# A decoder trunk on one core: four edits in the second attention joined, transposes moved, lambda loaded as columns, x ahead of the biases

## The reference

```python
mod = c_act @ ada_w[layer] + ada_b[layer]            # six vectors of 2048 for each layer
shift_t, scale_t, gate_t, shift_m, scale_m, gate_m = jnp.split(mod, N_MOD, axis=-1)
h = modulate(rms_norm(x, norm_g[layer, 0]), shift_t, scale_t)
# layer 0: dilated window attention; layer 1: differential attention on shared K and V
lam = jnp.exp(jnp.sum(lp[0] * lp[1])) - jnp.exp(jnp.sum(lp[2] * lp[3])) + lam_init
a = p[:, :, 0] - lam * p[:, :, 1]
x = x + gate_t[:, None, :] * y
h = modulate(rms_norm(x, norm_g[layer, 1]), shift_m, scale_m)
x = x + gate_m[:, None, :] * sq_relu_mlp(h, mlp_w1[layer], mlp_w2[layer])
```

## Time and profile before

| | us |
|---|---|
| median of 3 runs | 2373.57 (2373.55 to 2374.35) |
| profiled execution | 2374.41 |
| its span, first to last instruction | 2372.6 |
| PE busy in it | 2342.0 |
| VectorE busy | 1768.1 |
| ScalarE busy | 1242.7 |

### The profile page before, as it was taken

How to read it: one execution, slowest core, us unless ns; L and a number is a source line. 1 busy time by engine, 2 the same in 40 slices (tenths; PEclk the granted TensorE clock), 3 DMA queues, 4 the chain that set the end, 5 groups by cost and what they waited for, 6 DMA issues and landing times.

```text
span 2372.6 us, 28881 instructions
## 1 busy us (share of the span) xinstructions
PE 2342.0 (99%) x11309; PEld 1937.5 (82%) x11309; DVE 1768.1 (75%) x2291; ACT 1242.7 (52%) x2162; POOL 52.7 (2%) x74
## 2 busy tenths in 40 slices
PE   7999999999999999999999999999999999999999
PEld 4468888888888888888888888877888888888887
DVE  6678878888999878888898887858875555555554
ACT  3166566667535534534546666654653553553542
POOL 1000000001000000000001210000100000000000
PEclk9999999999999999999999999999999999999999
DMA  9987777966999888798886877657875555555554
GB/s 393 424 333 297 303 293 300 379 233 248 368 397 367 331 301 336 290 342 307 328 338 235 340 298 271 240 179 277 323 277 195 187 191 192 192 189 195 187 193 153
DMA packets 151000, 665.38 MB, mean 280 GB/s; under 512 B 17392, under 2 KB 17872, under 8 KB 121424
## 3 DMA queue, kind: packets, MB, share of 16 engines
q1 hardware_dynamic: 150864, 663.53, 75.0%
HBM read 661.33 MB, written 2.13 MB: 280 GB/s over the span
## 4 chain that ended last, share of the span: by engine, by line
PE 87%; DMA 5%; DVE 5%; ACT 3%; issue 1%; POOL 1%; SPq 0%; DVEq 0%; ACTq 0%
PE main L533 18%; PE main L428 16%; PE main L430 16%; PE main L429 16%; PE main L535 9%; DMA qT<-ada 3%; PE main L442 2%; PE main L444 2%; PE main L443 2%; DVE w_lo L1335 1%; DVE ada_raw L1342 1%; DMA subg_sb<-subg 1%; DVE qT L1342 1%; PE tr L584 1%; PE tr L533 1%
## 5 line engine op out<-in xcount | busy, mean ns | idle before, releaser
L906 ACT ACTIVATE w_hi<-w_raw 128x1024 fp32r<-128x1024 f32 x771 | 793.8, 1055 | 548.1 <-DMA w_raw<-w 545.0
L1335 DVE TENSOR_TENSOR w_lo<-w_raw,w_hi 128x1024 fp32r<-128x1024 f32 x771 | 921.6, 1220 | 213.1 <-ACT w_hi L906 211.0
L1342 DVE CUSTOM_DVE_ANT_0 ada_raw<-ada_raw,c_row,biasc 128x2048 f32<-128x2048 f32 x208 | 492.0, 2365 | 31.2 <-DMA ada_raw<-ada 30.0
L533 PE MATMUL main<-hT,w_hi 128*128 128x512 f32 x1856 | 464.7, 392 | 0.0
L533 PEld LDWEIGHTS main<-hT,w_hi 128*128 128x128 f32 x1856 | 334.3, 189 | 60.1
L428 PE MATMUL main<-w_hi,mid_hi 128*128 128x512 f32 x960 | 373.5, 389 | 0.0
L429 PE MATMUL main<-w_lo,mid_hi 128*128 128x512 f32 x960 | 373.5, 389 | 0.0
L430 PE MATMUL main<-w_hi,mid_lo 128*128 128x512 f32 x960 | 373.4, 389 | 0.0
L428 PE MATMUL main<-w_hi,hT 128*128 128x512 f32 x848 | 338.7, 399 | 1.8 <-ACTq L950 0.8
L430 PE MATMUL main<-w_hi,hT 128*128 128x512 f32 x848 | 330.8, 390 | 0.0
L429 PE MATMUL main<-w_lo,hT 128*128 128x512 f32 x848 | 330.1, 389 | 0.0
(11 more groups left out here) (270 smaller groups left out, 1884.2 us busy)
## 6 DMA issues: line engine op xcount, KB each, us to landing
w_raw<-w SPq DMA_DIRECT2D x800, 512.0 KB, 4.4
ada_raw<-ada SPq DMA_DIRECT2D x208, 1024.0 KB, 6.8
qT<-ada SPq DMA_DIRECT2D x16, 1024.0 KB, 12.3
gate<-gate_rows SPq DMA_DIRECT2D x4, 1024.0 KB, 8.3
xs<-x SPq DMA_DIRECT2D x1, 2048.0 KB, 7.6
out<-xs SPq DMA_DIRECT2D x3, 512.0 KB, 6.5
out<-xs SPq DMA_DIRECT2D x2, 256.0 KB, 2.6
st_a<-lamb SPq DMA_DIRECT2D x1, 256.0 KB, 17.9
```

The lines of the kernel that those rows point to most:

```text
L533: pe.matmul(banks[f][:, :], w_hi[:, s, wc], hT[:, :, kt, :], start=(kt == 0), stop=False)
L906: act.activation(w_hi[:, s, :], w_raw[:, s, :], ACT.Copy).then_inc(hi_done, 1)
L1335: dve.tensor_tensor(w_lo[:, s, :], w_raw[:, s, :], w_hi[:, s, :].bitcast(F32), ALU.subtract).then_inc(lo_done, 1)
L1342: dve.tensor_tensor_reduce(piece, piece, c_row[:, :], gain, biasc[:, section, kt:kt + 1], ALU.mult, ALU.add, out).then_inc(ada_used, 1)
```

## The change

**Second attention.** (1) No dots stand in V0 (`ADA_Q`, fifth list), V9 has three instead of two, V10 and V11 two each instead of three, and chunk B4 gets four (`ADA_GATE_B`). In the stream of dots all sections behind that move with them, so gate 2 is written and read in V4 instead of V2, and gate 3 in B4 and B5 instead of B4 (SyncE's `gate_steps`). The squares that ScalarE makes in Q3, for the norm of Q2's result (`qk_stats`, `ch == 3`), go to the banks `sc` and `ov` instead of `st_b`, and POOL waits for one root fewer before it writes `st_b`: the one in Q2 instead of the one in Q3. (2) `heads[2:4]` and `lows[2:4]` stand ahead of the split of piece V8.4 instead of behind it. (3) PE's transposes of heads 4 and 5 stand behind V8.2 instead of V8.1. (4) The table of the square root is loaded by an operation of its own ahead of `sub_stats` in V9.

**First chunks.** The first `qk_transposes` in A2 stand behind piece 2 instead of piece 1. x is loaded ahead of the biases. Lambda comes as 128 partitions by 4 elements; VectorE multiplies pairs, PE sums over the partitions with a matmul of `ones`, VectorE copies the two sums, and the two reductions in `angles` are gone. VectorE's last two copies of `c_row` stand ahead of the bias operations.

```diff
-ADA_Q = after((), (0, 5, 7), (0, 5, 7), (0, 5, 7), (0, 3, 6), (0, 5, 7), (0,))
-ADA_V = after((6, 7), (5, 7), (0, 6), (5, 7), (0, 6), (1, 2), (), (5, 6), (4, 5, 6), (0, 2, 5), first=2)
-ADA_GATE_B = after((1, 3, 5, 7), (0, 2, 4, 6), (0, 2, 4, 6))
+ADA_Q = after((), (0, 5, 7), (0, 5, 7), (0, 5, 7), (), (0, 5, 7), (0,))
+ADA_V = after((6, 7), (5, 7), (0, 6), (5, 7), (0, 6), (1, 2), (), (4, 5, 6), (4, 5), (0, 2), first=2)
+ADA_GATE_B = after((1, 3, 5, 7), (0, 2, 4, 6), (0, 2, 4, 6), (0, 1, 3, 4))
...
             sp.dma_start(cols_in[0:96, :], vecs_in).then_inc(vec_in, 16)
+            sp.dma_start(xs[:, :, :], x_in.rearrange("(t p) d -> p t d", p=P)).then_inc(x_in_done, 16)
             sp.dma_start(biasc[:, :, :], bias_cols_in).then_inc(bias_in, 16)
-            sp.dma_start(xs[:, :, :], x_in.rearrange("(t p) d -> p t d", p=P)).then_inc(x_in_done, 16)
+            sp.dma_start(lamb4[:, :], lamb_in).then_inc(lamb_in_done, 16)
...
-            sp.dma_start(st_a[:, 0:NC], lamb_in.partition_broadcast(P)).then_inc(small_in, 16)
...
-            gate_steps = {2: {3: lambda: gate_write(2), 6: lambda: gate_read(2, 4 + 16)}}
+            gate_steps = {4: {3: lambda: gate_write(2), 6: lambda: gate_read(2, 4 + 16)}}
...
-            gate_steps = {3: {1: lambda: gate_write(3), 4: lambda: gate_read(3, 4 + 16 + 4)}}
+            gate_steps = {3: {7: lambda: gate_write(3)}, 4: {1: lambda: gate_read(3, 4 + 16 + 4)}}
...
             spread_c()
+            pe.wait_ge(lamb_paired, 1)
+            claim_tr(0)
+            pe.matmul(tr[0][:, 0:2], ones[:, :], lamb2[:, :], start=True, stop=True).then_inc(lamb_summed, 1)
...
-                gemm(0, *h, side={1: [qk_transposes], 5: [qk_transposes]})
+                gemm(0, *h, side={2: [qk_transposes], 5: [qk_transposes]})
...
-                                  1: [head_transposes(4, heads), head_transposes(5, heads)],
+                                  2: [head_transposes(4, heads), head_transposes(5, heads)],
...
-                chunk(PIECES, {4: [qk_stats(1 - ch % 2)], 5: [qk_scale(1 - ch % 2)],
+                chunk(PIECES, {4: [qk_stats(1 - ch % 2, places=(sc, ov) if ch == 3 else None)], 5: [qk_scale(1 - ch % 2)],
...
-            chunk(PIECES, {3: heads[0:2], 4: [values(1), exps_of(0), exps_of(1)], 5: heads[2:4], 6: heads[4:6], 8: [move_pt]})
-            chunk(PIECES, {1: [sub_stats], 2: [sub_stats], 4: [heads[6]], 5: [heads[7]]})
+            chunk(PIECES, {3: heads[0:2], 4: [values(1), exps_of(0), exps_of(1), *heads[2:4]], 6: heads[4:6], 8: [move_pt]})
+            chunk(PIECES, {1: [load_sqrt, sub_stats], 2: [sub_stats], 4: [heads[6]], 5: [heads[7]]})
...
+            for q in range(2, 4):
+                dve.wait_ge(c_wide, q + 1)
+                dve.tensor_copy(c_row[:, cols(q, NC)], c_banks[q][:, :]).then_inc(c_spread, 1)
             dve.wait_ge(bias_in, 16)
...
-            for q in range(2, 4):
-                dve.wait_ge(c_wide, q + 1)
-                dve.tensor_copy(c_row[:, cols(q, NC)], c_banks[q][:, :]).then_inc(c_spread, 1)
+            dve.wait_ge(lamb_in_done, 16)
+            dve.tensor_tensor(lamb2[:, :], lamb4[:, 0::2], lamb4[:, 1::2], ALU.mult).then_inc(lamb_paired, 1)
+            dve.wait_ge(lamb_summed, 1)
+            dve.tensor_copy(lam[:, 0:2], tr[0][:, 0:2]).then_inc(tr_free[0], 1)
...
-                dve.wait_ge(small_in, 16 * 2)
-                lm = st_a[:, 0:NC].rearrange("p (a b) -> p a b", a=4)
-                dve.tensor_tensor_reduce(gate_flat[:, 0:P], lm[:, 0, :], lm[:, 1, :], 1.0, 0.0, ALU.mult, ALU.add, lam[:, 0:1])
-                dve.tensor_tensor_reduce(gate_flat[:, P:2 * P], lm[:, 2, :], lm[:, 3, :], 1.0, 0.0, ALU.mult, ALU.add,
-                                         lam[:, 1:2]).then_inc(lam_dot, 1)
+                dve.wait_ge(small_in, 16)
...
-            section_chunk(8, {2: [causal[0], negate_max(0)], 3: lows[0:2], 4: [causal[1], negate_max(1)], 5: [*lows[2:4], mix(0)], 6: [*lows[4:6], mix(1)],
+            section_chunk(8, {2: [causal[0], negate_max(0)], 3: lows[0:2],
+                              4: [causal[1], negate_max(1), *lows[2:4]], 5: [mix(0)], 6: [*lows[4:6], mix(1)],
...
-            modulate_kept((S_SCALE_KV, S_SHIFT_KV), 4 * PIECES, 4 * GROUPS + 3)
+            modulate_kept((S_SCALE_KV, S_SHIFT_KV), 4 * PIECES, 4 * GROUPS + 2)
```

More of the change, by code:

```diff
@@ L212, in trunk @@
         turns = sb("turns", [P, T * HALF])
+        lamb4 = sb("lamb4", [P, 4])
+        lamb2 = sb("lamb2", [P, 2])
         scratch = sb("scratch", [P, 1])
@@ L217, in trunk @@
         pos_i = sb("pos_i", [P, T], I32)
-        sb("skip", [P, 192])
+        sb("skip", [P, 186])
         with nc.sbuf_tensor("mid_hi", [P, KT, T * P], F32R) as mid_hi, \
@@ L263, in trunk @@
         ada_used = sem("ada_used")
+        lamb_in_done, lamb_paired, lamb_summed = sem("lamb_in_done"), sem("lamb_paired"), sem("lamb_summed")
         c_ready, c_wide, c_spread = sem("c_ready"), sem("c_wide"), sem("c_spread")
@@ L1679, in _ @@
             chained(last)
-            for q in range(2, 4):
-                dve.wait_ge(c_wide, q + 1)
-                dve.tensor_copy(c_row[:, cols(q, NC)], c_banks[q][:, :]).then_inc(c_spread, 1)
+            dve.wait_ge(lamb_in_done, 16)
+            dve.tensor_tensor(lamb2[:, :], lamb4[:, 0::2], lamb4[:, 1::2], ALU.mult).then_inc(lamb_paired, 1)
+            dve.wait_ge(lamb_summed, 1)
+            dve.tensor_copy(lam[:, 0:2], tr[0][:, 0:2]).then_inc(tr_free[0], 1)
+            dve.wait_ge(tr_free[0], 3)
+            dve.sem_inc(lam_dot, 1)
             dve.wait_ge(c_spread, 4)
@@ L2040 @@
         "subg": f["b_subln_g"].reshape(-1),
-        "lamb": f["b_lambda"].reshape(-1),
+        "lamb": f["b_lambda"].reshape(4, HD).T,
         "ada": np.concatenate([w.reshape(-1, D) for w in (first, *by_column[2:])]),
```

## The result

The changed kernel takes 2383.96 us (median of 5, 2382.15 to 2385.09) against 2373.57 (median of 5, 2372.58 to 2374.35): a ratio of 1.0043, 95% interval 1.0033 to 1.0054. It is 10.4 us slower. The prediction was 2362.2 with a range of 2359.5 to 2367.0, so it was wrong in sign and by 21.8 us.

A forecast was written before the change was run, and what follows sets the result against it. PE's work, taken as fixed, plus time in which PE starts no matmul bounds the kernel. Gains 1.2 + 1.6 + 1.6 + 1.4 + 1.2 + 4.4 = 11.4 us off 2374.4, less 0.84 for the median, give 2362.2 (2359.5 to 2367.0).

The forecast's parts named there:

- A: Start: smaller lambda load frees transfer time in the first stage; gain 1.2 us (-1.4 to 1.8), 1.05 by the 512 B rule.
- C: V0 to V1.1: no dots in V0 and POOL starting earlier regain 1.6 of 1.97 us lost, at least 0.8.
- F: V11: a dot less each in V10 and V11 removes PE's waits and the slow clock's 1.7; 4.4 us (1.0 to 4.8).
- B: A2: transposes one piece later remove PE's wait for the rope's last product; 1.6 us, or 0.4.
- D: V8: lows of heads 2 and 3 earlier, transposes of heads 4 and 5 later, remove PE's wait; 1.4 us, or 0.9.
- E: V9: square root table loaded ahead removes PE's wait for the seventh head's scaling; 1.2 us, or 0.8.
- R1: Rival, V9: SyncE stands at the block behind the added dot, weights land late, V9.7 waits; costs 4.0 us (2366.2), chance 0.17.
- R2: Rival: first stage is bound by its slots, so the later first dot makes A -1.4 us (2364.8); chance 0.10.
- R4: Rival, B4 to B5: gate 3 lands late and B5's first update waits, making the kernel slower (2379); chance 0.03.

The follow-up runs named there:

- e1: The changed kernel with filler `skip` at 170 elements instead of 186, so mid_hi and what follows start at the addresses of the kernel before; 2363.01 us, ratio 0.9955.
- e9: e1 with lambda loaded (256 KB to all partitions) and reduced as in the kernel before, x still ahead of the biases; 2365.26 us, ratio 0.9964.
- e12: e7 with the first qk_transposes of A2 behind piece 1 again instead of piece 2; 2361.01 us, ratio 0.9951 to the kernel before.
- e7: e1 with the added dot of V9 behind V9.0 instead of V9.4; 2360.59 us, ratio 0.9944 to the kernel before.
- e13: e7 with the dots' tables, places of the squares, POOL's root and the gates' places as in the kernel before; 2368.24 us, ratio 0.9977.
- e11: e7 with heads and lows 2 and 3 behind the split, transposes of heads 4 and 5 behind V8.1, the table loaded at the root; 2363.17 us, ratio 0.9959.
- e14: The kernel before with `skip` 16 elements shorter (176 instead of 192), mid_hi and mid_lo 64 bytes nearer to the weights; 2380.51 us, ratio 1.0027.
- e15: The kernel before with `skip` 48 elements longer (240 instead of 192), mid_hi and mid_lo 192 bytes further from the weights; 2380.22 us, ratio 1.0026.

## Why the prediction was wrong

**The step that failed** is in its first paragraph: "the time is PE's work plus the time in which PE doesn't start a matmul, and an edit on another engine is worth only what it takes out of that". The first summand was held fixed at 0.227 us for 512 columns. The change moved it to 0.233 for 3072 matmuls through two buffers of 16 and 8 bytes. No rival had it; "that the change doesn't do what it says has no room, since the order shows each edit" is the sentence that closed the door, for an order of instructions shows no address. The material was there: two new buffers and a filler whose only use is to place what follows, changed by the sum of their sizes. The range, 7.5 us wide, was made of waits alone. What the runs showed in its place: the 3072 matmuls on `mid_hi` and `mid_lo` cost 20.3 us more by their starts, 21 by e1. With the addresses right the time is 2363.0 (e1) against 2362.2. That it comes so near is in part luck, since errors of both signs cancel: A and C with F brought some 2.7 us more than forecast, B some 1 less, and the new wait cost 2.4.

Term by term, with the addresses right:

| term | forecast | measured | by |
|---|---|---|---|
| A, lambda | 1.2 (-1.4 to 1.8) | 2.25 | e9 against e1 |
| B, A2 | 1.6 (0.4 to 1.6) | 0.4 | e12 against e7 |
| C and F | 6.0 | 7.65 | e13 against e7 |
| D and E | 2.6 | 2.6 (2.9 between the traces) | e11 against e7 |
| R1, new wait | 0 (chance 0.17, 4.0) | -2.4 (-3.9 between the traces, with the clock's fall in e1) | e1 against e7 |
| placement | not seen | -21 | e1 against the changed kernel |

**A** was right in its mechanism and too small. The loss of rate was 1.2 us in one window, and I bounded the rest by lambda's own bytes; the trace of e9 shows a reduced rate in the window before too. From 16 to 20 us, e9 and then e1:

```profile
16.00:20.00 4.00, 2.19 (x10) 2.19 (x11) 3.96 (x6) 0.19 (x2) 0.00 (x0) 0.50 0.91 367
16.00:20.00 4.00, 1.34 (x6) 1.34 (x7) 3.96 (x6) 0.07 (x1) 0.00 (x0) 0.50 0.99 406
```

The two windows lack (39 + 124) GB/s x 4 us = 0.65 MB, or 1.5 us at 426 GB/s, and with the 0.6 of lambda's own bytes that makes 2.1 of the 2.25. R2 falls: the first dot came later (11.99 in the trace after, 13.11 in e1's, 11.77 before) without cost. I also read a row wrongly: 0.60 for "x5" is the time of all five bias operations, not of one; after, the same group takes 0.51. And the biases are 112 KB in the profile, not some 40. The sum for the delay came out near all the same: counted from the first copy of c_row, the first dot starts 1.44 later than before (3.24 against 1.80), through two hand-overs of 0.48 and 0.40 that I hadn't priced.

```profile
10.25 0.51 DVE L1686 SCALAR_TENSOR_TENSOR biasc<-biasc,vec 128x16 f32<-128x16 f32 x5
10.79 0.16 DVE L1690 TENSOR_TENSOR lamb<-lamb 128x2 f32<-128x2 f32 x1
11.43 0.16 DVE L1692 COPY lam<-tr 128x2 f32<-128x2 f32 x1 [0.48 <-PE tr L771]
11.99 2.35 DVE L1348 CUSTOM_DVE_ANT_0 ada_raw<-ada_raw,c_row,biasc 128x2048 f32<-128x2048 f32 x1 [0.40 <-DMA ada_raw<-ada]
```

The Trainium skill ("DMA: Bandwidth & Descriptors", Specifications) has 512 B as the least transfer for line rate. Here 2 KB in rows of 16 B took 7.2 us to land behind x's 2 MB, which cost the stage nothing visible, so no run tests the 0.15 us between 1.05 and 1.2; the measured 2.25 is above both.

**B** was wrong in size: the wait went, and most came back as PE had to wait later: 0.6 at 190 us for a split, and by the starts 0.3 more near 463 us, where the profile names no wait. The prediction asked what is late next for other terms and answered it here only up to the transposes' own users.

**C** was the full 1.95 of its bound in the trace after. **D** and **E** were right within the noise: 1.6 and 1.3 between the traces of e11 and e7, against 1.4 and 1.2. By the Trainium skill ("ScalarE: Activation LUTs", What ACT_TABLE_LOAD costs) E could have been worth up to 2.66. The trace doesn't agree: before, the load starts at 1581.17 and takes 1.28, and the root follows at once,

```profile
1582.47 0.30 ACT L1021 ACTIVATE rmsv<-ssv,eps_t 128x2 f32<-128x2 f32 x1
```

so the row's 1.28 was the price that counted.

**F** was right in place and cause, and measured 5.2 against 4.4. The addition of 1.7 for the clock was right in number by luck: e13 and e15 lose as much with a full clock, to a third wait of 1.7. The prediction took a fall of the clock as a cost of its own, without asking whether the next split was there.

**R1** happened, as a neighbour of what was written. SyncE did stand at the block (16.1 us) and the weights did come late. But the split of V9.7 was still in time; what was late was the update behind the splits of V10. The prediction held the chance at 0.17 against a margin of 0.2 us that it had worked out itself. Its price of 4.0 is met only where the clock falls too (3.9 in e1's trace).

R4 didn't happen; PE had no wait in B5.

## What to carry to other kernels

Before waits are counted, compare the start addresses of all buffers in the two built programs, and ask which matmuls read a pair whose distance changed. Before a slow clock is priced, ask whether what the engine needs next would have been there. A filler is kept right by the sizes as allocated (here 32 bytes for a buffer of 8), not by the sizes as written. And of a stream with two slots: a step put late into an idle chunk holds up whoever asks for the slot after the next, so a step belongs into the first idle time, not the last.

## What the runs showed of the hardware that I had not expected

- The pace of a matmul of 128x128 by 512 columns depends on where its two operands lie in the on-chip memory relative to each other. By the change of their distance modulo 256 bytes it was 226.8 ns at 0, 233.3 at 32 and 64, 232.4 at 128, 228.9 at 192 (in the last case 225.9, 229.1 and 231.7 for three kinds of pairs with the same distance modulo 256). Over this kernel that is up to 21 us, 0.9%.
- Moving all buffers together by 64 bytes leaves the matmuls alone.
- What a fall of the granted clock costs depends on what comes next. In V10 of e1, with the splits ready, 3.4 us at half clock cost 1.6 us. In V11, where the next split was late, they cost nothing: 18 matmuls in 6 us at 0.72 (e14) and at 1.00 (e15).
